# The first two blocks of values from the unscaled input, and the order of the first loads

## The chip, the cores and the metric

The kernel runs on one core of a Trainium2 chip. The metric is the time of one execution on the device in microseconds (us); lower is better. TensorE multiplies matrices, ScalarE and VectorE work on tiles in SBUF and PSUM, GpSimd does little here, and SyncE issues loads. TensorE's clock has two levels, 1.2 and 2.4 GHz; the profile tells which was granted.

## The reference

With the given sizes the model is one layer: a root-mean-square norm, one input projection, stick-breaking attention with 16 heads of 64, a gate, an output projection, the residual and a final norm.

```python
def rmsnorm(x, g):
    y = xf * lax.rsqrt(jnp.mean(xf * xf, axis=-1, keepdims=True) + EPS)
    return (y * g)
def mixer_stick_breaking(h, w_in, w_out):      # x: 2048 x 1024 float32, w_in: 1024 x 4096
    proj = jnp.einsum('bsd,de->bse', h, w_in)
    q, k, v, g = jnp.split(proj, 4, axis=-1)
    o = stick_breaking_attention(q.reshape(hs), k.reshape(hs), v.reshape(hs))
    return jnp.einsum('bse,ed->bsd', o * jax.nn.silu(g), w_out)
x = x + mixer_stick_breaking(rmsnorm(x, a_norm[j]), a_w_in[j], a_w_out[j])
return rmsnorm(x, final_norm)
```

## The kernel before

All products are made from high and low parts: a float32 tile a is split into a_hi (rounded for the matmul) and a_lo = a - a_hi, and a product is a_hi b_hi + a_hi b_lo + a_lo b_hi. ScalarE makes a high part, VectorE the low part from it.

**The value stage** comes first. The 2048 tokens are 16 blocks of 128 (NB), the model width 8 slices of 128 (KT). A value block v (32 of them: 16 token blocks times two halves of the 1024 value columns) is 8 x 3 matmuls of 128 x 512 into one of two PSUM tiles (proj_ps), lines 524 to 530. For token block s the stage needs:

- x_rows (x, line 376, two buffers), of which ScalarE takes the sum of squares (`square`), VectorE the mean (`mean`), ScalarE the root (`root`), and VectorE five small operations (`chain`) the scale of each token;
- `turn_scale`: TensorE multiplies the scale, broadcast along 128 columns, by the identity, so that it lies along the tokens in a spare PSUM tile;
- x_T (the transposed input, line 381, three buffers), which VectorE multiplies by the turned scale in place (`scaled`), and which is then split into hT_hi (`h_hi`) and hT_lo (`h_lo`). These stay for all later projections;
- the value weights, 8 slices in four quarters a half (wv_raw, line 384), multiplied by a_norm as they are split (`wv_high`, `wv_low`).

ScalarE copies a finished value block from PSUM to v_stage (`empty_v`, line 664) and issues its stores, one or two. The order of each engine's queue is written out by hand: after the first blocks all run in rounds s, in which ScalarE does root(s+2), h_hi(s), square(s+3), empty_v(s-2), and VectorE scaled(s), chain(s+2), h_lo(s), mean(s+3). TensorE's block v waits for h_lo(v) and for empty_v(v-2), and has turn_scale(v+2) in its middle. SyncE issues the loads in order, and waits where a buffer is not free:

```python
                def load_x(s):
                    if s >= 2:
                        sp.wait_ge(s_sumsq, s - 1)
                def load_xT(s):
                    if s >= 3:
                        sp.wait_ge(s_hlo, s - 2)
```

from block 4 on xT(s) and then x(s+1), with a quarter of the second half's weights after s = 7, 9, 11 and 13.

Behind it come the projections of queries, keys and gates, woven into 640 steps of attention, and the output (to 1715 us). Their instructions are not touched.

## Time and profile before

| | |
|---|---|
| median of 3 runs | 1716.97 us (1715.53 to 1718.01) |
| the profiled execution | 1717.58 us |
| its span, first to last instruction | 1715.6 us |
| TensorE busy | 1660.1 us (97%) |
| VectorE busy | 1307.8 us (76%) |
| ScalarE busy | 873.5 us (51%) |
| granted TensorE clock, mean | 0.991 of full |
| DMA | 216.08 MB, 126 GB/s on average |

Shares are averages over stages with different limits. The value stage is the first 204 us. A row of a timeline gives start and duration in us, engine, source line, operation, output and input, the number merged, and in brackets how long the engine stood idle before it and what ended that. Matmuls are pipelined: their durations overlap, so the pace is read from starts.

### The profile page before, as it was taken

What the parts mean: (1) busy time and instruction counts of PE and PEld (TensorE: products, weight loads), DVE (VectorE), ACT (ScalarE), POOL (GpSimd) and SP (SyncE); (2) the same over time, 40 slices, a digit from 0 to 9 for tenths busy, and PEclk for the clock granted to TensorE, in tenths of its full rate; (3) what the DMA queues carried; (4) which work ended last, traced back from release to release, by engine and by line L of the source; (5) the groups of instructions that cost most, each with busy time, mean ns of one, the idle gap of its engine ahead of it and who ended that gap; (6) DMA issues with size and microseconds to landing.
All of it is one profiled execution on the core that took longest, in us unless ns stands there. A gap on an engine that the chain in (4) does not pass through costs nothing. (4 is left out here: it accounts for less than half of the span.)

```text
span 1715.6 us, 23382 instructions
## 1 busy us (share of the span) xinstructions
PE 1660.1 (97%) x8600; PEld 1381.8 (81%) x8600; DVE 1307.8 (76%) x1855; ACT 873.5 (51%) x1730; POOL 230.0 (13%) x212
## 2 busy tenths in 40 slices
PE   5999999999999999999999999999999999989988
PEld 4778878888888888888888888888888888768776
DVE  5530058889888888888888888888888989955564
ACT  5431145556555565555565655555555656631221
POOL 0010012011111011201210211011101120003331
PEclk9999999999999999999999999999999999989999
DMA  6832243343524243333333341524243435456553
GB/s 247 277 97 50 70 135 119 115 118 95 157 69 136 65 149 94 105 99 111 109 101 111 99 142 57 147 85 134 81 119 105 115 96 177 142 178 227 200 199 110
DMA packets 156974, 216.08 MB, mean 126 GB/s; under 512 B 49088, under 2 KB 90048, under 8 KB 156864
## 3 DMA queue, kind: packets, MB, share of 16 engines
q1 hardware_dynamic: 87376, 139.05, 26.4%
q10 hardware_dynamic: 69488, 75.58, 14.7%
q8 instruction: 67, 1.10, 0.3%
q14 instruction: 43, 0.35, 0.1%
HBM read 139.01 MB, written 75.56 MB: 125 GB/s over the span
## 5 line engine op out<-in xcount | busy, mean ns | idle before, releaser
L711 ACT ACTIVATE u<-z_ps 128x512 f32<-128x512 f32 (+3 forms) x640 | 341.3, 533 | 413.8 <-PE z_ps L588 411.8
L885 DVE TENSOR_TENSOR_SCAN u<-u,u 128x512 f32<-128x512 f32 x384 | 490.8, 1278 | 0.0
L890 DVE TENSOR_TENSOR r_turned_lo<-turn_ps,r_turned_hi 128x512 fp32r<-128x512 f32 (+3 forms) x640 | 376.0, 588 | 35.4 <-ACT r_turned_hi L717 34.0
L717 ACT ACTIVATE r_turned_hi<-turn_ps 128x512 fp32r<-128x512 f32 (+3 forms) x640 | 339.8, 531 | 64.0 <-issue 45.0
L597 PE MATMUL turn_ps<-ident,u 128*128 128x128 f32 x2176 | 344.8, 274 | 0.0
L510 POOL TENSOR_SCALAR w_raw<-w_raw,a_norm_col 128x128 f32<-128x128 f32 x192 | 177.7, 943 | 1216.5 <-DMA w_raw<-in_w_qkg 1216.5
L570 PE MATMUL proj_ps<-hT_lo,w_hi 128*128 128x512 f32 x768 | 320.4, 417 | 0.0
L570 PE MATMUL proj_ps<-hT_hi,w_hi 128*128 128x512 f32 x768 | 320.1, 417 | 0.0
L570 PE MATMUL proj_ps<-hT_hi,w_lo 128*128 128x512 f32 x768 | 319.2, 416 | 0.0
L597 PEld LDWEIGHTS turn_ps<-ident,u 128*128 128x128 f32 x2176 | 269.3, 141 | 59.0 <-issue 0.4
L611 PE MATMUL o_ps<-r_turned_hi,dv_head 128*128 128x512 f32 (+3 forms) x640 | 233.2, 364 | 14.7 <-DVE r_turned_lo L890 13.1
L587 PE MATMUL z_ps<-k_parts,q_parts 128*128 128x512 f32 (+3 forms) x640 | 234.1, 366 | 0.3 <-ACT u L711 0.3
L588 PE MATMUL z_ps<-k_parts,q_swapped 128*128 128x512 f32 (+3 forms) x640 | 234.2, 366 | 0.0
L612 PE MATMUL o_ps<-r_turned_lo,dv_head 128*128 128x512 f32 (+3 forms) x640 | 232.9, 364 | 0.0
L885 DVE TENSOR_TENSOR_SCAN u<-u,unbroken 128x512 f32<-128x512 f32 (+3 forms) x256 | 210.1, 822 | 0.0
L611 PEld LDWEIGHTS o_ps<-r_turned_hi,dv_head 128*128 128x128 f32 x640 | 120.4, 188 | 51.9 <-DVE r_turned_lo L890 19.5
L570 PEld LDWEIGHTS proj_ps<-hT_hi,w_lo 128*128 128x128 f32 x768 | 145.5, 190 | 16.4
L570 PEld LDWEIGHTS proj_ps<-hT_lo,w_hi 128*128 128x128 f32 x768 | 145.6, 190 | 15.9
L570 PEld LDWEIGHTS proj_ps<-hT_hi,w_hi 128*128 128x128 f32 x768 | 145.4, 189 | 15.5
L871 DVE TENSOR_TENSOR made_lo<-proj_ps,made_hi 128x512 fp32r<-128x512 f32 x64 | 44.2, 690 | 144.9 <-ACT made_hi L692 144.9
L612 PEld LDWEIGHTS o_ps<-r_turned_lo,dv_head 128*128 128x128 f32 x640 | 120.8, 189 | 27.4
L587 PEld LDWEIGHTS z_ps<-k_parts,q_parts 128*128 128x128 f32 x640 | 120.4, 188 | 20.6 <-ACT u L711 1.0
(89 smaller groups left out, 1657.3 us busy)
## 6 DMA issues: line engine op xcount, KB each, us to landing
qk_hi_cols<-made_hi ACTq DMA_DIRECT2D x64, 256.0 KB, 2.8
qk_lo_cols<-made_lo ACTq DMA_DIRECT2D x64, 256.0 KB, 3.4
w_raw<-in_w_qkg SPq DMA_DIRECT2D x24, 512.0 KB, 3.6
x_rows<-in_x SPq DMA_DIRECT2D x16, 512.0 KB, 5.3
x_T<-in_xT SPq DMA_DIRECT2D x16, 512.0 KB, 4.4
v_rows<-v_stage ACTq DMA_DIRECT2D x32, 256.0 KB
v_here<-v_rows SPq DMA_DIRECT2D x64, 128.0 KB, 2.7
v_next<-v_rows SPq DMA_DIRECT2D x64, 128.0 KB, 2.9
```

The source lines that it names most:

```text
L510: last = nc.gpsimd.tensor_scalar(w_raw[t % 2][:, k, :], w_raw[t % 2][:, k, :], norm_col[:, k:k + 1], None, ALU.mult)
L570: last = nc.tensor.matmul(p_ps[g % RP][:], a[t % 2][:, k, :], b[:, c, k, :], start=(n == 0), stop=(n == QPM - 1))
L587: nc.tensor.matmul(out, q_parts[c % 2][:, tau], k_parts[:, sig], start=True, stop=False)
L588: nc.tensor.matmul(out, q_swapped[c % 2][:, tau], k_parts[:, sig], start=False, stop=True).then_inc(s_z, 1)
L597: last = nc.tensor.transpose(t_ps[m % RT][:, t * P:(t + 1) * P], u_t[unit][t][:, r * P - lo:(r + 1) * P - lo], ident[:])
L611: nc.tensor.matmul(o_ps[:, 0:w], weights, rt_hi[m % RT][:, 0:w], start=begin, stop=False)
L612: last = nc.tensor.matmul(o_ps[:, 0:w], weights, rt_lo[m % RT][:, 0:w], start=False, stop=end)
L711: nc.scalar.activation(u_t[(m // CB) % RU][STEPS[m][3]][:, 0:w], z_ps[m % RZ][:, 0:w], ACT.Sigmoid, scale=-Z_SCALE).then_inc(s_u, 1)
L717: nc.scalar.activation(rt_hi[m % RT][:, 0:w], t_ps[m % RT][:, 0:w], ACT.Copy).then_inc(s_hi, 1)
L871: nc.vector.tensor_tensor(made_lo[:], p_ps[g % RP][:], as_f32(made_hi[:]), ALU.subtract).then_inc(s_plo, 1)
L885: nc.vector.tensor_tensor_scan(u, u, other, start, ALU.mult, op).then_inc(s_r, 1)
L890: nc.vector.tensor_tensor(rt_lo[m % RT][:, 0:w], t_ps[m % RT][:, 0:w], as_f32(rt_hi[m % RT][:, 0:w]), ALU.subtract).then_inc(s_lo, 1)
```

## The change

For token blocks 0 and 1 (EARLY = 2) xT is split without the scale (`stage_hi`, `stage_lo`) into four new tiles, which lie where the second half's weights come later. Value blocks 0 and 1 are made from these, and ScalarE multiplies them by the token scale as it copies them out of PSUM (there the scale is one number a partition). The scaled parts of blocks 0 and 1 are still needed for value blocks 16 and 17 and for all other projections; they are made after those of block 2. `made(s)` is the place of block s in the order 2, 0, 1, 3, 4, .... The loads begin with xT(0), a_norm, the first quarter of the weights, xT(1), the other three quarters, and only then x(0) and x(1).

```diff
@@ -209,6 +209,17 @@
+EARLY = 2
+MADE = [EARLY] + list(range(EARLY)) + list(range(EARLY + 1, NB))
+def made(s):
+    return MADE.index(s) + 1
 CHAIN = 5
...
@@ -248,6 +259,8 @@
         xrow = [place(nc, f"x_rows{n}", [P, D], F32, at) for n, at in enumerate(AT_XROW)]
+        st_hi = [place(nc, f"unscaled_hi{n}", [P, KT, P], F32R, AT_WV[1][0] + 4 * KB * n) for n in range(EARLY)]
+        st_lo = [place(nc, f"unscaled_lo{n}", [P, KT, P], F32R, AT_WV[1][1] + 4 * KB * n) for n in range(EARLY)]
         vst = [place(nc, f"v_stage{n}", [P, HD], F32, AT_VST + 2 * KB * n) for n in range(2)]
...
@@ -302,6 +315,8 @@
         s_row = sem("scale_turned")
+        s_sthi = sem("unscaled_hi_ready")
+        s_stlo = sem("unscaled_lo_ready")
         s_scaled = sem("xT_scaled")
...
@@ -377,7 +392,7 @@
                     if s >= 3:
-                        sp.wait_ge(s_hlo, s - 2)
+                        sp.wait_ge(s_hlo, made(s - 3))
                     sp.dma_start(xt[s % 3][:], xT[s]).then_inc(s_xT[s % 3], 16)
...
@@ -414,17 +429,16 @@
-                load_x(0)
                 load_xT(0)
...
                 load_wv(0, 0)
+                load_xT(1)
+                for q in range(1, KT // 2):
+                    load_wv(0, q)
+                load_x(0)
                 load_x(1)
-                load_xT(1)
-                load_wv(0, 1)
-                load_wv(0, 2)
+                load_xT(2)
                 load_x(2)
-                load_wv(0, 3)
-                load_xT(2)
                 load_x(3)
...
@@ -432,6 +446,8 @@
                         load_x(s + 1)
+                    if s == 7:
+                        sp.wait_ge(s_v, EARLY)
                     if s in (7, 9, 11, 13):
...
@@ -517,35 +533,37 @@
                     if s >= len(row_ps):
-                        pe.wait_ge(s_scaled, s - len(row_ps) + 1)
+                        pe.wait_ge(s_scaled, made(s - len(row_ps)))
                     nc.tensor.transpose(row_ps[s % len(row_ps)][:, 0:P], scale[:, s:s + 1].to_broadcast([P, P]),
...
                     f, (c, tok) = v // NB, block_of(v % NB)
+                    hi, lo = (hT_hi[:, c, :, tok], hT_lo[:, c, :, tok]) if v >= EARLY else (st_hi[v][:], st_lo[v][:])
                     for k in ks:
-                        for n, (a, b) in enumerate(((hT_hi, wv_hi[f]), (hT_hi, wv_lo[f]), (hT_lo, wv_hi[f]))):
-                            last = nc.tensor.matmul(p_ps[v % 2][:], a[:, c, k, tok], b[:, k, :],
+                        for n, (a, b) in enumerate(((hi, wv_hi[f]), (hi, wv_lo[f]), (lo, wv_hi[f]))):
+                            last = nc.tensor.matmul(p_ps[v % 2][:], a[:, k, :], b[:, k, :],
                                                     start=(k == 0 and n == 0), stop=(k == KT - 1 and n == 2))
...
                 pe.wait_ge(s_ident, 2)
-                turn_scale(0)
-                turn_scale(1)
                 for q in range(KT // 2):
                     pe.wait_ge(s_wvlo, q + 1)
-                    for v in range(2):
+                    for v in range(EARLY):
                         if q == 0:
-                            pe.wait_ge(s_hlo, v + 1)
+                            pe.wait_ge(s_stlo, v + 1)
                         last = products(v, range(2 * q, 2 * q + 2))
...
                             last.then_inc(s_v, 1)
-                    if q >= 2:
-                        turn_scale(q)
-                for v in range(2, 2 * NB):
+                            if v == 0:
+                                for s in range(EARLY + 1):
+                                    turn_scale(s)
+                turn_scale(EARLY + 1)
+                for v in range(EARLY, 2 * NB):
                     if v < NB:
-                        pe.wait_ge(s_hlo, v + 1)
+                        pe.wait_ge(s_hlo, made(v))
                     if v == NB:
+                        pe.wait_ge(s_hlo, NB)
                         pe.wait_ge(s_wvlo, KT)
...
@@ -647,8 +665,12 @@
                     c, tok = block_of(s)
-                    act.wait_ge(s_scaled, s + 1)
+                    act.wait_ge(s_scaled, made(s))
                     nc.scalar.activation(hT_hi[:, c, :, tok], xt[s % 3][:], ACT.Copy).then_inc(s_hhi, 1)
+                def stage_hi(s):
+                    act.wait_ge(s_xT[s % 3], 16)
+                    nc.scalar.activation(st_hi[s][:], xt[s % 3][:], ACT.Copy).then_inc(s_sthi, 1)
...
@@ -661,7 +683,11 @@
                         v_stored(act, v - 2)
-                    nc.scalar.activation(vst[v % 2][:], p_ps[v % 2][:], ACT.Copy).then_inc(s_vst, 1)
+                    if v < EARLY:
+                        act.wait_ge(s_chain, CHAIN * (v + 1))
+                        nc.scalar.activation(vst[v % 2][:], p_ps[v % 2][:], ACT.Copy, scale=scale[:, v:v + 1]).then_inc(s_vst, 1)
+                    else:
+                        nc.scalar.activation(vst[v % 2][:], p_ps[v % 2][:], ACT.Copy).then_inc(s_vst, 1)
                     act.wait_ge(s_vst, v + 1)
...
@@ -743,26 +769,25 @@
-                square(0)
-                root(0)
-                square(1)
-                root(1)
+                stage_hi(0)
                 act.wait_ge(s_norm, 16)
                 wv_high(0, 0)
+                stage_hi(1)
+                for q in range(1, KT // 2):
+                    wv_high(0, q)
+                for s in range(EARLY + 1):
+                    square(s)
+                    root(s)
+                h_hi(EARLY)
+                square(EARLY + 1)
                 h_hi(0)
-                wv_high(0, 1)
+                root(EARLY + 1)
                 h_hi(1)
-                wv_high(0, 2)
-                square(2)
-                wv_high(0, 3)
-                root(2)
-                square(3)
-                root(3)
-                square(4)
+                square(EARLY + 2)
                 for s in range(2, 2 * NB + 2):
...
                         root(s + 2)
-                    if s < NB:
+                    if EARLY < s < NB:
                         h_hi(s)
...
@@ -833,9 +858,13 @@
                     c, tok = block_of(s)
-                    dve.wait_ge(s_hhi, s + 1)
+                    dve.wait_ge(s_hhi, made(s))
                     nc.vector.tensor_tensor(hT_lo[:, c, :, tok], xt[s % 3][:], as_f32(hT_hi[:, c, :, tok]),
                                             ALU.subtract).then_inc(s_hlo, 1)
+                def stage_lo(s):
+                    dve.wait_ge(s_sthi, s + 1)
+                    nc.vector.tensor_tensor(st_lo[s][:], xt[s % 3][:], as_f32(st_hi[s][:]), ALU.subtract).then_inc(s_stlo, 1)
...
@@ -906,24 +935,26 @@
                 nc.vector.memset(zeros[:], 0.0).then_inc(s_zero, 1)
-                mean(0)
-                chain(0)
-                mean(1)
-                chain(1)
+                stage_lo(0)
+                wv_low(0, 0)
+                stage_lo(1)
+                for q in range(1, KT // 2):
+                    wv_low(0, q)
+                for s in range(EARLY + 1):
+                    mean(s)
+                    chain(s)
+                scaled(EARLY)
                 scaled(0)
-                wv_low(0, 0)
+                h_lo(EARLY)
+                scaled(1)
+                mean(EARLY + 1)
                 h_lo(0)
-                scaled(1)
-                wv_low(0, 1)
+                chain(EARLY + 1)
                 h_lo(1)
-                wv_low(0, 2)
-                mean(2)
-                wv_low(0, 3)
-                chain(2)
-                mean(3)
-                chain(3)
-                mean(4)
-                for s in range(2, NB):
+                mean(EARLY + 2)
+                chain(EARLY + 2)
+                mean(EARLY + 3)
+                for s in range(EARLY + 1, NB):
                     scaled(s)
...
                         chain(s + 2)
```

**ScalarE, from the squares of block 2 or 3 to the first copy out of PSUM.** Before (x_T_66 is block 2; v_stage_69 takes value block 0; the x_rows alternate, so the last squares ahead of the copy are block 5's):

```order
L642 ACTIVATE square_junk,stat<-x_rows_67 128x1024 [waits sum_squares_ready,x_loaded0]
L646 ACTIVATE stat<-stat 128x1 [waits mean_square_ready]
L651 ACTIVATE hT_hi<-x_T_66 128x8x128 [waits xT_scaled]
L642 ACTIVATE square_junk,stat<-x_rows_68 128x1024 [waits sum_squares_ready,x_loaded1]
L664 ACTIVATE v_stage_69<-proj_ps 128x512 [waits v_ready]
L668 DMA v_rows<-v_stage_69 128x8x64 [waits v_evacuated]
L646 ACTIVATE stat<-stat 128x1 [waits mean_square_ready]
```

and with the change, from the squares of block 2 on:

```order
L660 ACTIVATE square_junk,stat<-x_rows_67 128x1024 [waits sum_squares_ready,x_loaded0]
L664 ACTIVATE stat<-stat 128x1 [waits mean_square_ready]
L669 ACTIVATE hT_hi<-x_T_66 128x8x128 [waits xT_scaled]
L660 ACTIVATE square_junk,stat<-x_rows_68 128x1024 [waits sum_squares_ready,x_loaded1]
L669 ACTIVATE hT_hi<-x_T_64 128x8x128 [waits xT_scaled]
L664 ACTIVATE stat<-stat 128x1 [waits mean_square_ready]
L669 ACTIVATE hT_hi<-x_T_65 128x8x128 [waits xT_scaled]
L660 ACTIVATE square_junk,stat<-x_rows_67 128x1024 [waits sum_squares_ready,x_loaded0]
L664 ACTIVATE stat<-stat 128x1 [waits mean_square_ready]
L660 ACTIVATE square_junk,stat<-x_rows_68 128x1024 [waits sum_squares_ready,x_loaded1]
L688 ACTIVATE v_stage_73<-proj_ps,token_scale 128x512 [waits rms_chain,v_ready]
L694 DMA v_rows<-v_stage_73 128x8x64 [waits v_evacuated]
```

Squares 2, 3 and 4 stood ahead of the high part of block 2 and only squares 5 behind it; now the high parts of blocks 2, 0 and 1 (x_T_66, x_T_64, x_T_65) and squares 3, 4 and 5 all stand between squares 2 and the copy of block 0.

**SyncE, the loads after the first ones.** Before, from x(2) to x(5):

```order
L376 DMA x_rows_67<-in_x 128x1024 [waits sum_squares_ready]
L384 DMA wv_raw_62<-in_w_v 128x1024
L381 DMA x_T_66<-in_xT 128x1024
L376 DMA x_rows_68<-in_x 128x1024 [waits sum_squares_ready]
L381 DMA x_T_64<-in_xT 128x1024 [waits hT_lo_ready]
L376 DMA x_rows_67<-in_x 128x1024 [waits sum_squares_ready]
L381 DMA x_T_65<-in_xT 128x1024 [waits hT_lo_ready]
L376 DMA x_rows_68<-in_x 128x1024 [waits sum_squares_ready]
```

and with the change, from the last three quarters of the first weights to x(4) and xT(4):

```order
L399 DMA wv_raw_62<-in_w_v 128x1024 x3
L391 DMA x_rows_67<-in_x 128x1024
L391 DMA x_rows_68<-in_x 128x1024
L396 DMA x_T_66<-in_xT 128x1024
L391 DMA x_rows_67<-in_x 128x1024 [waits sum_squares_ready]
L391 DMA x_rows_68<-in_x 128x1024 [waits sum_squares_ready]
L396 DMA x_T_64<-in_xT 128x1024 [waits hT_lo_ready]
L391 DMA x_rows_67<-in_x 128x1024 [waits sum_squares_ready]
L396 DMA x_T_65<-in_xT 128x1024 [waits hT_lo_ready]
L391 DMA x_rows_68<-in_x 128x1024 [waits sum_squares_ready]
```

x(0) and x(1) moved behind all first weights. The first x_T that waits (x_T_64, block 3) waits for the low part of block 0, which is now the second made.

**VectorE and TensorE behind the scales.** VectorE with the change, from the end of the third chain:

```order
L857 TENSOR_TENSOR x_T_66<-x_T_66,turn_ps 128x1024 [waits scale_turned,xT_loaded2,rms_chain]
L857 TENSOR_TENSOR x_T_64<-x_T_64,z_ps 128x1024 [waits scale_turned,xT_loaded0]
L862 TENSOR_TENSOR hT_lo<-x_T_66,hT_hi 128x8x128 [waits hT_hi_ready]
L857 TENSOR_TENSOR x_T_65<-x_T_65,z_ps 128x1024 [waits scale_turned,xT_loaded1]
L847 TENSOR_SCALAR stat<-stat 128x1 [waits sum_squares_ready]
L862 TENSOR_TENSOR hT_lo<-x_T_64,hT_hi 128x8x128 [waits hT_hi_ready]
```

TensorE with the change, from the last matmul of value block 0:

```order
L545 MATMUL proj_ps<-wv_hi_58,unscaled_lo_71 128x512
L537 MATMUL z_ps<-ident,token_scale 128x128 [waits rms_chain] x2
L537 MATMUL turn_ps<-ident,token_scale 128x128 [waits rms_chain]
L545 MATMUL proj_ps<-wv_hi_58,unscaled_hi_70 128x512
L545 MATMUL proj_ps<-wv_lo_60,unscaled_hi_70 128x512
```

The low part of block 0 is the sixth of these operations, and the scales of blocks 0, 1 and 2 are turned between the value blocks 0 and 1, where before the turns of 0 and 1 came ahead of all products.

## Rows read from the trace of the kernel before

**Rows 1.** Busy time by stretch (us, engines, TensorE clock, DMA share, GB/s).

```profile
30.49:60.00 29.51, 28.11 (x123) 22.32 (x124) 17.13 (x41) 14.05 (x25) 0.00 (x0) 1.00 0.86 263
93.00:106.00 13.00, 13.00 (x52) 10.41 (x53) 8.15 (x13) 5.65 (x9) 0.00 (x0) 0.87 0.42 103
106.00:203.80 97.80, 97.80 (x433) 81.00 (x432) 4.67 (x5) 14.15 (x22) 9.31 (x16) 1.00 0.25 60
```

**Rows 2.** Who waited for whom, TensorE, whole span (us in total, times, longest).

```profile
PE proj_ps L528 <- ACT v_stage L664: 6.4, 6, 1.8
```

**Rows 3.** Timeline of TensorE: first matmuls of blocks 0, 2 and 12.

```profile
15.71 0.77 PE L528 MATMUL proj_ps<-wv_hi,hT_hi 128*128 128x512 f32 x1 [3.33 <-DVE hT_lo L837]
...
30.49 0.47 PE L528 MATMUL proj_ps<-wv_hi,hT_hi 128*128 128x512 f32 x1 [1.23 <-ACT v_stage L664]
...
92.86 0.47 PE L528 MATMUL proj_ps<-wv_hi,hT_hi 128*128 128x512 f32 x1 [1.80 <-ACT v_stage L664]
```

**Rows 4.** Timeline of ScalarE, 28.5 to 31.5 us and at 203.8.

```profile
28.73 1.04 ACT L642 ACTIVATE square_junk<-x_rows 128x1024 bf16<-128x1024 f32 x1
...
29.77 0.57 ACT L664 ACTIVATE v_stage<-proj_ps 128x512 f32<-128x512 f32 x1
...
30.86 0.20 ACT L646 ACTIVATE stat<-stat 128x1 f32<-128x1 f32 x1 [0.52 <-ACT v_stage L664]
31.38 1.06 ACT L651 ACTIVATE hT_hi<-x_T 128x1024 fp32r<-128x1024 f32 x1 [0.31 <-DVE x_T L832]
...
203.85 0.60 ACT L664 ACTIVATE v_stage<-proj_ps 128x512 f32<-128x512 f32 x1 [4.84 <-PE proj_ps L528]
```

**Rows 5.** Who waited for whom, ScalarE, 30 to 106 us.

```profile
ACT square_junk L642 <- DMA x_rows<-in_x: 15.4, 8, 3.3
```

**Rows 6.** Timeline of VectorE: the low parts of blocks 0, 1, 2, 3 and 4.

```profile
14.34 1.22 DVE L837 TENSOR_TENSOR hT_lo<-x_T,hT_hi 128x1024 fp32r<-128x1024 f32 x1
...
17.93 1.22 DVE L837 TENSOR_TENSOR hT_lo<-x_T,hT_hi 128x1024 fp32r<-128x1024 f32 x1
...
28.93 1.23 DVE L837 TENSOR_TENSOR hT_lo<-x_T,hT_hi 128x1024 fp32r<-128x1024 f32 x1 [0.35 <-ACT hT_hi L651]
...
32.95 1.22 DVE L837 TENSOR_TENSOR hT_lo<-x_T,hT_hi 128x1024 fp32r<-128x1024 f32 x1 [0.76 <-ACT hT_hi L651]
...
40.39 1.23 DVE L837 TENSOR_TENSOR hT_lo<-x_T,hT_hi 128x1024 fp32r<-128x1024 f32 x1
```

**Rows 7.** Timeline of SyncE, 30 to 31 us.

```profile
30.18 0.33 SPq L381 DMA_DIRECT2D x_T<-in_xT  x1
30.55 0.43 SPq L376 DMA_DIRECT2D x_rows<-in_x  x1
```

**Rows 8.** DMA issues between 30.1 and 30.9 us: KB, us to landing.

```profile
x_T<-in_xT SPq DMA_DIRECT2D x1, 512.0 KB, 3.8
x_rows<-in_x SPq DMA_DIRECT2D x1, 512.0 KB, 5.2
```

**Rows 9.** DMA issues between 0.7 and 1.2 us.

```profile
x_rows<-in_x SPq DMA_DIRECT2D x1, 512.0 KB, 3.6
```

**Rows 10.** DMA issues between 5.95 and 6.5 us.

```profile
wv_raw<-in_w_v SPq DMA_DIRECT2D x1, 512.0 KB, 9.6
```

**Rows 11.** Timeline of ScalarE, 5 to 12 us.

```profile
5.60 1.28 ACT L646 ACT_TABLE_LOAD   x1
6.89 0.20 ACT L646 ACTIVATE stat<-stat 128x1 f32<-128x1 f32 x1
9.23 1.06 ACT L642 ACTIVATE square_junk<-x_rows 128x1024 bf16<-128x1024 f32 x1 [2.13 <-DMA x_rows<-in_x]
...
10.78 1.32 ACT L656 ACTIVATE wv_hi<-wv_raw,a_norm_col 128x512 fp32r<-128x512 f32 x2
```

**Rows 12.** Timeline of VectorE, 11 to 15 us.

```profile
11.68 0.16 DVE L226 TENSOR_TENSOR token_scale<-token_scale,stat 128x1 f32<-128x1 f32 x1
...
13.02 1.41 DVE L843 SCALAR_TENSOR_TENSOR wv_lo<-wv_raw,a_norm_col,wv_hi 128x512 fp32r<-128x512 f32 x2
```

## The prediction

> **What bounds the kernel now.** I read the stretches first, then who waited for whom, then the timelines around the places where TensorE stood. From 106 to 203.8 us TensorE never rests: 433 matmuls in 97.8 us, 0.226 us each, so a value block of 24 costs 5.42 us [rows 1]. That is the pace it could hold throughout. From 30.49 to 60 us it is busy for only 28.11 of 29.51 us [rows 1]. In the whole span TensorE waits 6.4 us, in 6 waits, for the copies of values out of PSUM (v_stage, line 664) [rows 2]. It begins its first block at 15.71, block 2 at 30.49 and block 12 at 92.86 us [rows 3]; the last block leaves PSUM at 203.85 [rows 4]. From 30.49 to 92.86 are 10 blocks, 6.24 us each, against 5.42. After 92.86 it is only TensorE. So **the end of the value stage is set by when block 12 may start**, and all later work follows it one for one.
>
> Who sets the 6.24? ScalarE's queue. In round s it does root(s+2), the high part of block s, the squares of block s+3, and only then empties block s-2 [rows 4]. The squares wait for rows of x: 15.4 us in 8 waits between 30 and 106 us [rows 5]. The rows come late because SyncE's queue is in order: x(s+3) stands behind xT(s+2), which waits for the low part of block s-1, whose buffer it takes. The low part of block 2 ends at 30.15 (28.93 + 1.22) [rows 6]; xT(5) and x(6) are issued at 30.18 and 30.55 [rows 7] and land 3.8 and 5.2 us later [rows 8]. So there is a loop: h_lo(s-1), load x(s+3) 5.6, squares 1.0, empty 0.6 with its DMA issues 1.1, root and high part 1.2, low part 1.2 gives h_lo(s+1). That makes 11 to 12 us for two blocks: h_lo ends at 30.15, 34.17 and 41.62 [rows 6], 11.5 from the first to the third. Two such chains, of even and odd blocks, take turns.
>
> **The change, part by part.**
> - Loads. Nine loads of 512 KB, with the small a_norm between them, land between 4.4 us (0.8 + 3.6) [rows 9] and 15.6 (6.0 + 9.6) [rows 10]: one per 1.4. In the new order the places are xT(0) 4.4, the four quarters of the weights and xT(1) up to 11.5, x(0) about 13, x(1) 14.2, xT(2) 15.6.
> - First products. Splitting xT(0) costs 1.06 + 1.22, the first weights 1.32 on ScalarE and 1.41 on VectorE [rows 6, 11, 12]. Weights landed at 6.6 give a start near 9 to 9.5 us instead of 15.71, 6 us earlier. 48 matmuls, some eight of them at the lower clock, and the turns: both blocks are done by 23 us, before by 29.3 (block 2's start less its wait of 1.23) [rows 3].
> - Scales. They now come last. Squares of x(0) end at 14.2, the table load takes 1.28 [rows 11], squares of x(1) end near 17. x(2) can't be issued before 14.2 and lands 3.6 later, 17.8. From the start of its squares to the end of its chain takes 2.6 (9.23 to 11.84) [rows 11, 12]: 20.5. That meets TensorE after block 0 (42 matmuls from 9.4: 20.7), so the wait put between block 0 and block 1 is 0 to 0.5 us, hidden by what follows.
> - Blocks 0 and 1 still need scaled parts for the later projections, and now they are made behind block 2's. VectorE has scaled(2), scaled(0), low(2), scaled(1), low(0), five passes of 1.15 and a wait of 1.0 for ScalarE's high part, from 21.1: **h_lo(0) ends near 27.5** (before 15.56), h_lo(1) a chain and a pass later, 29.7 (before 19.15) [rows 6].
> - What that frees. xT(3) waits for h_lo(0), x(4) is queued behind it: issued at 27.9, landed at 32.7 (xT(3) 3.8 after its issue at 27.5 and one place of 1.4; the 5.2 of rows 8 has a store of values beside it, here none is out yet). Behind it stand xT(4), released at 29.7, and x(5): two more places, 35.4. In the kernel before, x(4) and x(5) were long there.
> - The emptying of block 0 stands behind squares(4) and squares(5) on ScalarE. 35.4 + 1.04 + 0.57 and 0.15 to TensorE (30.49 against 29.77 + 0.57) [rows 3, 4]: **block 2 starts near 37.0 instead of 30.49, 6.5 us later**. So the 6 us won at the start lie in front of a wait of some 14 us (23 to 37, broken only by the turn of scale 3) and are worth nothing.
> - How it goes on. mean(5) now stands ahead of scaled(3) on VectorE, so h_lo(3) follows squares(5): 36.6, scaled 1.2, high 1.1, low 1.2, near 40.2 (before 34.17, +6.0). h_lo(4) follows the emptying of block 1, near 44.3 (before 41.62, +2.7) [rows 6]. These are the starts of the two chains. Their loads share one queue, so the later one pushes the other: the shift settles between 2.7 and 6.0. I take 4.5, the middle, since block 12 waits for x(15), whose place in the queue both have touched; that puts block 12 near 97.4 instead of 92.86. If TensorE alone decided, block 2 plus ten at 5.42 would put block 12 at 91.2; the loop's 6.24 is longer, so the loop decides.
> - The new scaled copy of v_stage replaces a plain one twice, and the wait ahead of the next load of weights is long met when it comes: nothing.
>
> The sum: 4.5 us on top of the profiled execution's 1717.58, whose span is 1715.6: 1722.1. That run is 0.6 above the median of 1716.97, so **1721.5**.
>
> A rule to weigh. The table load is 1.28 us, from 5.60, with the root right behind it at 6.89, and it stands now on the way to x(1)'s squares [rows 11]. The Trainium skill (ScalarE: Activation LUTs, What ACT_TABLE_LOAD costs) gives 1283 ns and another 1380 ns of drain per switch. By that the squares of x(1) would end at 18.3 instead of 17, 0.5 past the landing of x(2), and the estimate would be 0.5 us more; the trace shows no such second part.
>
> **The rivals.**
> 1. The shift is mostly swallowed: 0 to 3.4 us, about 1719. The less delayed chain (+2.7) decides, or the fall of the clock between 93 and 106 us (0.87 on average over 13 us, so 1.7 us lost [rows 1]) does not come again. For: both are of the size. Against: h_lo(3) is far behind and its chain feeds the same queue.
> 2. Faster: from block 2 on TensorE sets the pace. Needs the loads to keep up, since without the early loads nothing is squeezed together: x(4) and x(5) each 3.6 us after their issue and block 2 at 35.3. Then 30 blocks of 5.42 and 1.7 at the lower clock end at 199.6 against 203.8, 4.2 less, 1713. It decides if the loop's round falls under 5.42. Against: it is 6.24 now, and the same loads, passes and copies stand in it.
> 3. Slower by more: 7 to 10 us, 1725. Over 14 us of waiting the clock falls to 1.2 GHz and block 2 starts there; as rows 1 show for 93 to 106 us it costs 1.7, which delays the turn of scale 4 and with it h_lo(4), and both chains run at +6. The Trainium skill (TensorE: Matmul & The Clock Gate, HAM oscillation) says that waiting for DMA brings the engine back to the slow clock, burst after burst; by that I would add 1.7 for each further long wait. Before, the first waits of 1.2 us did not show a lower clock in the row of 30.49 to 60 us.
> 4. The change does not start the products early, because the weights land no sooner. The end stays as worked out: the path does not run through them.
>
> **How the numbers follow.** A measurement here can tell about 0.2%, 3.4 us, from no change. The forecast (+3.4 to +7) gets 0.62, rival 1 0.23, rival 2 0.07, rival 3 0.08. Faster 0.06, since rival 2 can fall short of 3.4; same 0.24; slower 0.70. The range that holds 8 in 10 reaches from +0.8 into rival 1 to +8.5 into rival 3: 1717.8 to 1725.5.
>
> **What would show it.** First product near 9.4 us; squares(4) and squares(5) waiting for x; xT(3) issued near 27.5; block 2 near 37; then 5.4 to 6.3 us a block, and the last v_stage near 208. Wrong if the last v_stage is at or before 204, or if block 2 starts before 33.

## The result, and the profile after

| | before | with the change |
|---|---|---|
| median of 5 runs | 1717.13 us (1715.53 to 1719.57) | 1725.10 us (1724.06 to 1730.15) |
| ratio | | 1.0051, 95% interval 1.0034 to 1.0069 |
| profiled execution | 1717.58 us | 1724.06 us |
| its span | 1715.6 us | 1722.3 us |

Slower by 8.0 us, half a per cent, where 4.5 were forecast. The way was right and the size was not: 1725.1 is just inside the range given, but the ratio of 1.0051 on 1716.97 is 1725.7 and just outside it. All times and ratios below are of fast runs: one execution each of e3, e8 and e10 took 1900 to 2765 us at a much lower granted clock and is left out.

The stretches of the new kernel (columns as in [rows 1]): ahead of the start of block 2, from there until the loads end, and TensorE alone.

```profile
10.83:40.25 29.42, 14.28 (x53) 11.04 (x53) 17.26 (x45) 16.01 (x28) 0.00 (x0) 0.81 0.56 205
40.25:106.00 65.75, 63.17 (x267) 50.72 (x268) 38.19 (x91) 32.73 (x58) 0.00 (x0) 0.95 0.77 229
114.00:211.50 97.50, 97.50 (x432) 80.77 (x431) 5.09 (x5) 14.45 (x23) 9.30 (x16) 1.00 0.25 60
```

From 114 us on it is the pace of before, 432 matmuls in 97.5 us. The first stretch holds 14.28 us of work in 29.42 and a mean clock of 0.81. Who waited for whom on TensorE [rows 2], the whole span:

```profile
PE proj_ps L545 <- DVE wv_lo L872: 10.8, 1, 10.8
PE proj_ps L545 <- ACT v_stage L688: 9.6, 1, 9.6
...
PE turn_ps L537 <- DVE token_scale L237: 5.5, 1, 5.5
PE proj_ps L545 <- ACT v_stage L690: 2.6, 2, 1.8
```

One wait of 9.6 us for the copy of block 0 (line 688) and one of 5.5 for the fourth scale take the place of the small ones. The timeline of TensorE at those places [rows 3]:

```profile
10.83 0.76 PE L545 MATMUL proj_ps<-wv_hi,unscaled_hi 128*128 128x512 f32 x1 [10.83 <-DVE wv_lo L872]
...
22.96 0.27 PE L537 MATMUL turn_ps<-ident,token_scale 128*128 128x128 f32 x1
...
30.16 0.48 PE L537 MATMUL turn_ps<-ident,token_scale 128*128 128x128 f32 x1 [5.54 <-DVE token_scale L237]
40.25 0.76 PE L545 MATMUL proj_ps<-wv_hi,hT_hi 128*128 128x512 f32 x1 [9.61 <-ACT v_stage L688]
```

Block 0 starts 4.9 us earlier than before, block 2 9.8 us later. Block 12 stands behind the last such wait:

```profile
102.12 0.47 PE L545 MATMUL proj_ps<-wv_hi,hT_hi 128*128 128x512 f32 x1 [1.81 <-ACT v_stage L690]
```

9.3 us later than in [rows 3]. ScalarE at the squares of x(0), x(4), x(5), the copy of block 0, and the last copy [rows 4]:

```profile
14.34 1.06 ACT L660 ACTIVATE square_junk<-x_rows 128x1024 bf16<-128x1024 f32 x1
...
34.42 1.06 ACT L660 ACTIVATE square_junk<-x_rows 128x1024 bf16<-128x1024 f32 x1 [5.11 <-DMA x_rows<-in_x]
...
38.38 1.06 ACT L660 ACTIVATE square_junk<-x_rows 128x1024 bf16<-128x1024 f32 x1 [2.38 <-DMA x_rows<-in_x]
...
39.43 0.67 ACT L688 ACTIVATE v_stage<-proj_ps,token_scale 128x512 f32<-128x512 f32 x1
```

```profile
211.56 0.60 ACT L690 ACTIVATE v_stage<-proj_ps 128x512 f32<-128x512 f32 x1 [4.84 <-PE proj_ps L545]
```

Squares(4) and (5) wait 5.11 and 2.38 us for their rows of x, and the copy of block 0, ready since 23 us, is behind them. The last copy is at 211.56 instead of 203.85: **the value stage is 7.7 us longer, and that is the whole effect.** What follows took 1510.7 us here and 1511.7 before.

Of the 9.3 us at block 12, 1.6 are won back behind it, because the kernel before has a stretch at the lower clock there (94.2 to 97.7 us) and the changed one has none. And from block 4 to block 10 TensorE waits for nothing. The first row is the changed kernel over blocks 4 to 9, 5.59 us each and no idle time; the other two are the kernel before, over blocks 4 to 8 and over blocks 9 to 11:

```profile
54.39:87.95 33.56, 33.56 (x151) 27.38 (x150) 20.11 (x45) 17.11 (x30) 0.00 (x0) 1.00 0.85 250
43.26:71.67 28.41, 28.24 (x126) 22.68 (x125) 15.61 (x40) 14.24 (x26) 0.00 (x0) 1.00 0.97 298
71.67:92.86 21.19, 17.45 (x76) 13.38 (x75) 12.64 (x29) 10.51 (x19) 0.00 (x0) 1.00 0.59 190
```

So the 6.24 us a block of the prediction are a mean. TensorE's own pace with a turn in each block is 5.59; before, 3.7 of the waits stand ahead of blocks 10, 11 and 12, and 1.23 each ahead of blocks 2 and 3. ScalarE's waits for x [rows 5], 30 to 106 us:

```profile
ACT square_junk L660 <- DMA x_rows<-in_x: 17.5, 9, 5.1
```

VectorE's low parts [rows 6], in the order 2, 0, 1, 3, 4, and the scaling of block 4:

```profile
25.71 1.22 DVE L862 TENSOR_TENSOR hT_lo<-x_T,hT_hi 128x1024 fp32r<-128x1024 f32 x1
...
28.05 1.22 DVE L862 TENSOR_TENSOR hT_lo<-x_T,hT_hi 128x1024 fp32r<-128x1024 f32 x1
...
30.14 1.23 DVE L862 TENSOR_TENSOR hT_lo<-x_T,hT_hi 128x1024 fp32r<-128x1024 f32 x1
...
42.15 1.23 DVE L862 TENSOR_TENSOR hT_lo<-x_T,hT_hi 128x1024 fp32r<-128x1024 f32 x1 [0.35 <-ACT hT_hi L669]
...
46.02 1.22 DVE L857 TENSOR_TENSOR x_T<-x_T,z_ps 128x1024 f32<-128x1024 f32 x1 [2.58 <-PE z_ps L537]
...
48.44 1.22 DVE L862 TENSOR_TENSOR hT_lo<-x_T,hT_hi 128x1024 fp32r<-128x1024 f32 x1 [0.35 <-ACT hT_hi L669]
```

h_lo(0) ends at 29.27 and h_lo(1) at 31.37 (before 15.56 and 19.15), h_lo(3) at 43.38 and h_lo(4) at 49.66. SyncE acts on each at once [rows 7]:

```profile
29.29 0.33 SPq L396 DMA_DIRECT2D x_T<-in_xT  x1
29.66 0.43 SPq L391 DMA_DIRECT2D x_rows<-in_x  x1
31.40 0.33 SPq L396 DMA_DIRECT2D x_T<-in_xT  x1
31.77 0.43 SPq L391 DMA_DIRECT2D x_rows<-in_x  x1
```

and the landings of the last pair (xT(4) and x(5)) [rows 8]:

```profile
x_T<-in_xT SPq DMA_DIRECT2D x1, 512.0 KB, 5.7
x_rows<-in_x SPq DMA_DIRECT2D x1, 512.0 KB, 6.6
```

### The profile page after: what moved, and what is told of

Read it like the earlier page. It is cut to its first block and busy times, and to the rows that moved or that the text cites. A ratio compares the mean times of both kernels' runs of the same rounds, so it can differ in the third digit from the quotient of the medians.

```text
span 1722.3 us, 23387 instructions
## 1 busy us (share of the span) xinstructions
PE 1660.1 (96%) x8600; PEld 1382.8 (80%) x8600; DVE 1313.3 (76%) x1857; ACT 876.6 (51%) x1732; POOL 231.5 (13%) x212
## 5 line engine op out<-in xcount | busy, mean ns | idle before, releaser
L630 PEld LDWEIGHTS o_ps<-r_turned_lo,dv_head 128*128 128x128 f32 x640 | 120.8, 189 | 27.5
```

Source lines behind the costliest of these rows:

```text
L630: last = nc.tensor.matmul(o_ps[:, 0:w], weights, rt_lo[m % RT][:, 0:w], start=False, stop=end)
```

## The experiments

Each kernel was timed against the kernel before. Since one execution's remainder behind the value stage varies by some us (1510.7 to 1516.0 over the profiled executions here) whatever was edited, the place of the last copy out of PSUM in the value stage tells an edit better than the total; the one kernel profiled twice (e7 and e7b) gave 198.72 and 198.37. Only the kernel before has the stretch at the lower clock behind block 12: from the start of block 12 to the last v_stage it takes 111.0 us, all others 109.3 to 109.4, so against the kernel before the start of block 12 compares better. The start of block 0 too varies, from 9.5 to 11.1 us over the kernels that keep the change's first loads, with the landing of the first weights.

| kernel | block 0 starts | block 2 starts | h_lo(3), h_lo(4) end | block 4 starts | block 12 starts | last v_stage | ratio to before (95%) |
|---|---|---|---|---|---|---|---|
| before | 15.71 | 30.49 | 34.17, 41.62 | 43.26 | 92.86 | 203.85 | 1 |
| the change | 10.83 | 40.25 | 43.38, 49.66 | 54.39 | 102.12 | 211.56 | 1.0051 (1.0034 to 1.0069) |
| e1 loads only | 22.65 | 37.47 | 41.16, 48.61 | 50.25 | 100.77 | 210.20 | 1.0051 (1.0034 to 1.0069) |
| e2 x first | 10.90 | 39.99 | 43.12, 48.51 | 52.94 | 101.89 | 211.31 | 1.0030 (1.0016 to 1.0043) |
| e3 empty first | 10.08 | 28.98 | 42.19, 45.80 | 50.57 | 98.55 | 207.98 | 1.0018 (1.0005 to 1.0031) |
| e4 two x ahead | 10.22 | 33.15 | 36.28, 45.41 | 47.03 | 96.55 | 205.98 | 0.9997 (0.9987 to 1.0008) |
| e5 keep clock | 11.09 | 40.08 | 43.20, 49.49 | 54.08 | 102.33 | 211.74 | 1.0039 (1.0028 to 1.0050) |
| e5b clock kept | 10.96 | 39.76 | 42.89, 47.39 | 51.03 | 99.69 | 209.12 | 1.0030 (1.0017 to 1.0042) |
| e6 turns earlier | 10.64 | 38.26 | 41.39, 46.59 | 51.04 | 99.16 | 208.57 | 1.0013 (1.0003 to 1.0023) |
| e7 rows first, before | 16.15 | 33.36 | 37.06, 41.04 | 44.67 | 89.41 | 198.72 | 0.9959 (0.9944 to 0.9974) |
| e7b the same again | 15.80 | 33.05 | 36.74, 40.72 | 44.32 | 89.06 | 198.37 | 0.9954 (0.9940 to 0.9968) |
| e8 rows first, change | 10.23 | 34.91 | 38.04, 44.33 | 48.77 | 93.52 | 202.82 | 0.9990 (0.9980 to 1.0000) |
| e9 late xT(4), before | 15.75 | 39.07 | 42.62, 48.50 | 53.15 | 101.46 | 210.87 | 1.0033 (1.0022 to 1.0044) |
| e10 repaired change | 9.50 | 28.31 | 36.26, 40.85 | 42.08 | 86.83 | 196.13 | 0.9957 (0.9943 to 0.9971) |

From block 4 to block 12 the kernels with the old order of x(s+1) and xT(s) take 47.7 to 50.5 us, and those with the new one (e7, e7b, e8, e10) 44.7. So an edit ahead of block 4 shows at block 12 within 2 us as it shows at block 4.

### e1: the new order of the loads, alone

```diff
 # before.py, SyncE
-load_x(0); load_xT(0); norm; load_wv(0, 0); load_x(1); load_xT(1); load_wv(0, 1); load_wv(0, 2); load_x(2); load_wv(0, 3); load_xT(2)
+load_xT(0); norm; load_wv(0, 0); load_xT(1); load_wv(0, 1..3); load_x(0); load_x(1); load_xT(2); load_x(2)
```

> The kernel before with nothing but the new order of the first loads. Theory L (the late scales of blocks 0 and 1 shift the loop of x loads): x(0) lands at 14.3 instead of 4.4, so the scales of blocks 0 and 1 and their low parts come some 7 to 10 us late; block 0 starts near 22, block 2 near 36.5, the last v_stage near 210 (the change: 211.6), 5 to 7 us slower than before. Rival P (what hurts is that the unscaled blocks push the scaled parts of 0 and 1 and the turns behind them, and the order of the loads is harmless): last v_stage within 1 us of 203.9.

Last v_stage 210.20: the loads alone cost 6.4 of the 7.7 us (at block 12, 7.9 of 9.3). TensorE waits 17.4 us for the first scale:

```profile
PE z_ps L520 <- DVE token_scale L226: 18.4, 2, 17.4
PE proj_ps L527 <- ACT v_stage L663: 7.1, 5, 1.8
```

### e2: the change, x(0) and x(1) first in the loads

```diff
 # after.py, SyncE
+load_x(0); load_xT(0); norm; load_wv(0, 0); load_x(1); load_xT(1); load_wv(0, 1..3); load_xT(2); load_x(2)
```

> The change with x(0) first again in the loads (x(0), xT(0), a_norm, a quarter, x(1), xT(1), three quarters, xT(2), x(2)). Theory L: ScalarE does its squares behind all weights whatever has landed, and the weights land one or two places later, so the squares of x(2) and h_lo(0) come at the same time or up to 1 us later than in the change: block 2 near 40 to 41, last v_stage 211 to 213. Rival (the order of the loads alone costs the 7.7 us): last v_stage near 204 to 206.

211.31, as the change. So the two parts don't add: each alone makes the scales late, the loads because x lands late, ScalarE's order because the squares stand behind the weights (here the squares of x(0) start at 15.66 us, right behind the last weights, though its load was the first). Giving back one of them gives back nothing.

### e3: blocks 0 and 1 copied out ahead of the squares that wait

```diff
 # after.py, ScalarE
                 h_hi(1)
+                empty_v(0)
                 square(EARLY + 2)
...
+                    if s == 2:
+                        empty_v(1)
                     if s + 3 < NB:
                         square(s + 3)
-                    empty_v(s - 2)
+                    if s > 3:
+                        empty_v(s - 2)
```

> The change with blocks 0 and 1 copied out of PSUM ahead of squares(4) and squares(5) on ScalarE. Theory L: block 2 starts near 31 instead of 40.3, 9 us earlier, and the last v_stage stays within 1.5 us of 211.6, since the loop of x loads sets block 12. Rival E (the wait of 9.6 us ahead of block 2 is itself the loss): the last v_stage comes 6 to 9 us earlier, near 203 to 205.

Block 2 starts 11.3 us earlier and the stage ends 3.6 earlier, of which up to 0.75 may be the earlier start of this execution. Neither figure holds: more than the 1.5 that I allowed, far less than the wait of 9.6. TensorE's time comes back as new waits, first for the scale of block 4, whose squares wait for x(4), then for h_lo(3):

```profile
28.85 0.48 PE L537 MATMUL turn_ps<-ident,token_scale 128*128 128x128 f32 x1 [5.53 <-DVE token_scale L237]
...
35.86 0.32 PE L537 MATMUL z_ps<-ident,token_scale 128*128 128x128 f32 x1 [1.43 <-DVE token_scale L237]
...
42.24 0.79 PE L545 MATMUL proj_ps<-wv_hi,hT_hi 128*128 128x512 f32 x1 [3.30 <-DVE hT_lo L866]
```

The wait of 3.30 us for h_lo(3), which itself is only 1.2 us earlier, and a lower clock in blocks 2 and 3 (0.61 on average from 28.98 to 35.80, 0.66 from 42.20 to 50.57) leave 3.8 us at block 4 (50.57 instead of 54.39), and these reach the end. So an early block 2 alone is lost again at block 3, whose low part hangs on the late loads.

### e5 and e5b: TensorE kept busy in its wait

```diff
 # after.py, TensorE
+                for _ in range(32):                    # e5b: 48
+                    nc.tensor.transpose(t_ps[2][:, 0:P], ident[:], ident[:])
                 turn_scale(EARLY + 1)
+                for _ in range(56):                    # e5b: 86
+                    nc.tensor.transpose(t_ps[2][:, 0:P], ident[:], ident[:])
```

> The change with 32 and 56 transposes of the identity into an unused PSUM tile where TensorE waits between blocks 1 and 2 (extra work, no result of it is used), so that its clock stays up. Theory L: the turn of scale 4 in the middle of block 2 comes 2.6 us earlier and h_lo(4) with it (47 instead of 49.7), but the last v_stage moves by less than 1 us from 211.6, since the other chain of loads is as late. Rival C (the lower clock after the long wait is what made the loss larger than forecast): last v_stage 2 to 3 us earlier, near 209.

The edit missed its aim: the transposes ran out at 36.5 us, TensorE stood 3.54 us more, its clock was low from 39.1 us, and block 2 ran slow as without them. It serves as the control for the next run, with more of them:

> As the run with the 32 and 56 transposes, where TensorE still stood 3.5 us ahead of block 2 and its clock was low from 39.1 to 45.9 us; now 48 and 86, which fill the wait. Theory L: if the clock stays up, the turn of scale 4 comes 2.6 us after the start of block 2 instead of 5.3, h_lo(4) near 47, and the last v_stage still within 1 us of 211.6. Rival C (the clock's cost is carried through): last v_stage 2 to 3 us earlier, near 209.

Now the clock stays at 2.4 GHz through block 2, and the turn of scale 4 comes 2.8 us after the start of block 2 (39.76); the scaling of block 4 follows at 42.95, not at 46.02:

```profile
39.76 0.47 PE L546 MATMUL proj_ps<-wv_hi,hT_hi 128*128 128x512 f32 x1
...
42.57 0.27 PE L538 MATMUL z_ps<-ident,token_scale 128*128 128x128 f32 x1
```

```profile
42.95 1.22 DVE L862 TENSOR_TENSOR x_T<-x_T,z_ps 128x1024 f32<-128x1024 f32 x1
...
46.16 1.23 DVE L867 TENSOR_TENSOR hT_lo<-x_T,hT_hi 128x1024 fp32r<-128x1024 f32 x1
```

The stage ends 2.4 us earlier (2.6 against e5): **rival C holds**, and my theory's "within 1 us" falls. Block 2 takes 5.68 us instead of 8.55 (first row the change, second e5b):

```profile
40.25:48.80 8.55, 8.55 (x26) 6.74 (x26) 4.99 (x15) 4.13 (x7) 0.00 (x0) 0.64 0.67 185
39.76:45.44 5.68, 5.68 (x26) 4.64 (x27) 4.18 (x11) 3.41 (x7) 0.00 (x0) 1.00 0.41 110
```

These 2.9 us, and 0.5 of an earlier start of block 2, are still there in full at block 9 (79.00 instead of 82.36), since TensorE waits for nothing between; the waits ahead of blocks 10 to 12 take 0.9 of the 3.4 back. The early turn is thus not what carries it: from block 3 to block 9 every low part is ready 2.5 us or more ahead of its block, in both kernels. The ratio, 1.0030 against 1.0051, has intervals that overlap.

### e6: the turns of the scales ahead of block 0's last quarter

```diff
 # after.py, TensorE
                     for v in range(EARLY):
+                        if (q, v) == (KT // 2 - 1, 0):
+                            for s in range(EARLY + 1):
+                                turn_scale(s)
...
-                            if v == 0:
-                                for s in range(EARLY + 1):
-                                    turn_scale(s)
```

> The change with the turns of the scales of blocks 0, 1 and 2 ahead of the last quarter of block 0 on TensorE instead of behind it. In the change the third turn ran at 22.96 us, 1.5 us after its scale was ready (21.44), and the scaled blocks began at 23.37. Theory L: h_lo(0) and all behind it come 1.3 to 1.5 us earlier, and so does the last v_stage: 210.0 to 210.5. Rival (this step has slack): last v_stage within 0.5 us of 211.6, counted from the same start of block 0.

The third turn runs at 21.23 after a wait of 0.30, h_lo(0) ends at 27.59, 1.7 us earlier, and the stage ends 3.0 earlier, twice what was expected. This step had no slack. What makes 3.0 of it shows in block 2: it starts 2.0 us earlier (38.26), and it takes 7.18 us instead of 8.55, because the clock is back at 2.4 GHz 3.1 us after its start and not 6.2:

```profile
38.26:45.44 7.18, 7.18 (x25) 5.72 (x26) 4.71 (x15) 4.14 (x7) 0.00 (x0) 0.78 0.61 157
```

Of these 3.4 us 3.0 reach block 12.

### e4: x(4) and x(5) ahead of the transposed block 3

```diff
 # after.py, SyncE
                 load_x(3)
-                load_xT(3)
                 load_x(4)
+                load_x(5)
+                load_xT(3)
                 for s in range(4, NB):
                     load_xT(s)
-                    if s + 1 < NB:
+                    if 4 < s < NB - 1:
```

> The change with x(4) and x(5) issued ahead of xT(3), which waits for h_lo(0). Theory L: x(4) and x(5) land near 25 and 31 instead of 34.4 and 38.4, block 2 starts near 34 instead of 40.3, and this shift stays: the last v_stage near 207.5 (3.5 to 5 us less than 211.6). Rival (the late transposed blocks xT(3) and xT(4) themselves hold the stage, not the rows queued behind them): last v_stage within 1 us of 211.6.

205.98: 5.6 of the 7.7 us come back, a little more than the 3.5 to 5 expected, with two loads moved past one that waits. Nothing was saved in work or bytes.

### e9: one late load, put into the kernel before

```diff
 # before.py, SyncE, load_xT
-                        sp.wait_ge(s_hlo, s - 2)
+                        sp.wait_ge(s_hlo, 3 if s == 4 else s - 2)
```

> The kernel before, in which only xT(4), and x(5) behind it, waits for the low part of block 2 (30.2 us) instead of that of block 1 (19.2). Theory L: this one wait repeats the harm: x(5) lands near 36, block 2 starts near 37 instead of 30.5, last v_stage 4 to 6 us later, near 208 to 210. Rival (the harm needs the unscaled blocks, the clock or the new order of operations): last v_stage within 1 us of 203.9.

210.87, 7.0 us later (8.6 at block 12), more than the 4 to 6 expected, with the first products and all queues of the engines as before. As in the change, the clock falls in the long wait and block 2 takes 8.48 us, so this run shows the late load and the slow block that comes of it together. TensorE's wait is the change's in small:

```profile
PE proj_ps L528 <- ACT v_stage L664: 10.3, 3, 7.3
```

A load that waits, with the rows of x behind it in SyncE's queue, is enough for the harm.

### e7 and e8: x(s+1) ahead of xT(s) throughout

```diff
 # before.py (e7) and after.py (e8), SyncE
                 load_x(3)
-                load_xT(3)
                 load_x(4)
+                load_xT(3)
                 for s in range(4, NB):
-                    load_xT(s)
                     if s + 1 < NB:
                         load_x(s + 1)
+                    load_xT(s)
```

> The kernel before with x(s+1) issued ahead of xT(s) from s = 3 on, nothing else. Theory L (x behind xT behind the low part makes the round of 6.2 us a block): the waits for x on ScalarE nearly go, TensorE runs at 5.44 us a block, block 12 starts near 87.5 instead of 92.9, the last v_stage near 197 to 198.5 and the time 5 to 7 us below the kernel before. Rival (the DMA engines are full in this stage, so x only trades places with xT): last v_stage within 1.5 us of 203.9.

198.72 and 0.9959 of the kernel before, 7 us below it. From block 2 to block 12 it takes 5.6 us a block, not the 5.44 that I expected (the turn in the middle of each block costs TensorE the rest), and block 12 starts at 89.41, 3.45 us earlier, though block 2 started 2.9 later. Of the 6.3 us by which these ten blocks are shorter, 4.4 lie in blocks 9 to 11, where the waits of the kernel before stand; at the last v_stage 1.6 more come from its stretch at the lower clock, which does not occur here. Behind a single wait of 1.23 us at block 2 TensorE waits for no copy any more; from 30 to 106 us ScalarE waits for x no more, and for the scaled block instead, which TensorE's pace sets:

```profile
PE proj_ps L528 <- ACT v_stage L664: 1.2, 1, 1.2
```

```profile
ACT hT_hi L651 <- DVE x_T L832: 22.4, 11, 4.7
```

> The change with x(s+1) issued ahead of xT(s) from s = 3 on. Theory L: x(4) comes early but x(5) still waits its turn, block 2 near 37 to 38, then TensorE's own pace: last v_stage near 204 to 205, so 7 us below the change and about level with the kernel before, and 6 to 7 us above the kernel before with the same edit. Rival (the start 5 us earlier is now worth something, because the pace is TensorE's): last v_stage at or below that of the kernel before with this edit, 197.

202.82: 8.7 us below the change and 4.1 above e7; I had expected 204 to 205, 6 to 7 above e7, with block 2 at 37 to 38. With a start 5.9 us earlier than e7's, block 2 still begins 1.6 later, and from there neither waits. The other 2.5 us are the clock: in e8 it is low until 40.5 us, and block 2's first thirteen matmuls take 0.43 us each instead of 0.23 (the first row is e8 from the start of block 2, the second e7):

```profile
34.91:40.50 5.59, 5.59 (x14) 4.32 (x15) 2.70 (x8) 3.04 (x6) 0.00 (x0) 0.51 0.88 266
```

```profile
33.36:40.00 6.64, 6.64 (x30) 5.41 (x31) 4.96 (x15) 4.23 (x8) 0.00 (x0) 1.00 0.81 260
```

### e10: the change with everything mended

```diff
 # after.py with e3, e6 and
                 load_x(3)
+                load_x(4)
+                load_x(5)
                 load_xT(3)
-                load_x(4)
...
+                scaled(EARLY + 1)
                 mean(EARLY + 3)
                 for s in range(EARLY + 1, NB):
-                    scaled(s)
+                    if s > EARLY + 1:
+                        scaled(s)
```

and x(s+1) ahead of xT(s) for s > 4.

> The change with all that the runs found: x(s+1) ahead of xT(s), x(5) ahead of xT(3), the turns of 0 to 2 ahead of block 0's last quarter, blocks 0 and 1 copied out ahead of squares(4) and (5), scaled(3) ahead of the mean of block 5. Theory L: block 2 starts near 28.5 to 29.5, but block 3 still waits for h_lo(3), near 36 to 37, since x(4) and the scale of block 3 come late; last v_stage 199 to 201, 0 to 2 us behind the kernel before with rows first (198.7). Rival (the start 5 us earlier pays once the loads are out of the way): last v_stage below 197.

> The kernel before with x(s+1) ahead of xT(s), once more on the same chip as the repaired change: last v_stage 198 to 199, 5 to 8 us below the kernel before.

196.13 against 198.37 for e7b, in times 1712.5 and 1712.1 us (medians), and ratios 0.9957 and 0.9954. In the stage my theory (199 to 201) fell and its rival held (below 197: the early start pays once the loads are out of the way); in the whole time nothing shows, since 2.2 us are less than the executions of either kernel differ by (4.9 and 6.1 us). Block 0 of e10 started 0.6 us earlier than in any other kernel with its loads, and that may be part of the 2.2. A first product 6.3 us earlier returns 2.2 at most, and only with four other edits; the order of two loads returned 5.1 and 5.5 alone. The theory had block 3 right, which waits for h_lo(3) at 36.3:

```profile
36.31 0.50 PE L546 MATMUL proj_ps<-wv_hi,hT_hi 128*128 128x512 f32 x1 [0.56 <-DVE hT_lo L867]
```

## Why the prediction was wrong

- **That the early start is worth nothing**, because x(4), x(5) and with them block 2 come late behind loads that wait for a buffer: right. Block 0 started 4.9 us earlier and nothing of it was left in the end, and e9 repeats the harm without it.
- **"The loop's 6.24 is longer, so the loop decides"**: this step failed as a mechanism. It compares 6.24, a mean over ten blocks with all their waits, with 5.42, TensorE's pace without turns. With its turns TensorE takes 5.59 a block, and in the change nothing holds it up between the start of block 2 and block 10; the loop of loads tells only ahead of block 2 and again from 10 to 12. So the late block 2 is not evened out between two chains but carried on: block 4 starts 11.1 us later than before, block 9 10.7, block 12 9.3. In size this step erred least: a block 2 at 37.0 with the clock up, followed by the 59.0 us that the change takes from there to block 12 without the 2.9 of the slow block, gives 96.0, 3.1 later than before, where the sum had 4.5.
- **The start near 9 to 9.5**: 10.83. The first weights landed at 7.8 us (issued at 1.72, 6.1 us), not at 6.6, and all that lands later came with them: x(0) at 14.3 (4.29 + 10.0) instead of 13, x(2) at 18.8 instead of 17.8. This term was a uniform 1.4 us per place; the first places took longer.
- **"0 to 0.5 us, hidden by what follows"** for the wait between blocks 0 and 1: wrong in sign and size. The scale was ready at 21.44, and the turn stood behind block 0's last matmuls until 22.96. It delayed VectorE by 1.5 us, and e6 shows that nothing hid it: 3.0 us at the end.
- **h_lo(0) near 27.5, h_lo(1) 29.7**: 29.27 and 31.37, 1.8 and 1.7 late, by the two terms above.
- **x(4) at 32.7, x(5) at 35.4**: 34.4 (when the squares begin) and 38.37 (31.77 + 6.6). The first is late with h_lo(0). For the second I gave xT(4) one place of 1.4; it took 5.7 us from its issue, with no store beside it.
- **Block 2 near 37.0**: 40.25, the sum of these: 3.3 us, the largest term that was mis-sized.
- **The lower clock, priced at 1.7 us in rival 3 and at nothing in the sum**: the step that failed in size. At the start of block 2 the granted clock was low, for the 12 matmuls of 0.43 us up to the turn and two behind it, and the block took 2.9 us more than at 2.4 GHz (e5b: 5.68 instead of 8.55). I gave rival 3 only 0.08, and let it work through the turn of scale 4. h_lo(4) did come at 49.66 instead of 44.3, 3.3 us from block 2's late start and some 2 from the clock; but no block waited for it, and the loss went through TensorE's own time. The Trainium skill (TensorE: Matmul & The Clock Gate, HAM oscillation), cited in that rival, has waits for DMA bring the slow clock back. The trace agrees for the long waits ahead of block 2. The waits of 1.8 us further on are shorter than those it describes, and went both ways: the clock stayed up behind the one of 1.81 at 102 us, and before it fell behind one of 1.80 at 92.86.
- **The shift settles between +2.7 and +6.0, so 4.5**: it was +9.8 at block 2 and +9.3 at block 12. The middle of two chains was no rule, and its two ends were 5.3 and 3.2 us short (+8.0 and +9.2 measured for h_lo(4) and h_lo(3)). The sum that the runs give is 3.1 (above), 3.3 for the later block 2 and 2.9 for the clock, 9.3 at block 12, less the 1.6 of the stretch at the lower clock that only the kernel before has behind it: 7.7.
- Rival 1 had one half right: the fall of the clock between 93 and 106 us did not come again, and the stage ended only 7.7 us later where block 12 was 9.3 later. Of rival 2 the condition held (from block 2 on TensorE set the pace, up to block 10), but from a block 2 that came 9.8 us late, so nothing was gained.
- The table load: 1.28 us, from 15.51, and the root at 16.80, as before. The second part that the Trainium skill (ScalarE: Activation LUTs, What ACT_TABLE_LOAD costs) adds does not show here either:

```profile
15.51 1.28 ACT L664 ACT_TABLE_LOAD   x1
16.80 0.20 ACT L664 ACTIVATE stat<-stat 128x1 f32<-128x1 f32 x1
```

## What to carry to other kernels

An engine that starts earlier gains only if what it waits for next comes earlier too; find the last wait ahead of the stretch that runs without waits, and follow it back through the buffers that are given free, not only through the data. In an in-order queue of loads, one that waits for a buffer holds up all behind it, so the load whose buffer comes free first belongs first: that swap alone was worth 0.4%. Before a mean round is called the pace of a loop, look at the blocks one by one: here most ran at TensorE's own pace and a few held all the waits. And a long new wait on TensorE has to be priced with the slow block behind it, 2.9 us here, which nothing takes back as long as TensorE sets the pace.

## What the runs showed of the hardware that was not expected

- Three loads of 512 KB issued within 0.9 us at 31.4 us took 5.7, 6.6 and 7.4 us, while the pair issued from 29.29 on took 3.9 and 4.7. The first store of values was issued only at 40.13; what slowed the three was not tried.
- 56 transposes of 128 x 128 until 36.5 us and a wait of 3.54 did not keep the clock of block 2 up; 86 that ran into it did. In the change it fell at 29.4 us, 4.7 us after TensorE's last matmul of block 1, and was low until 46.4.
- The same first loads started block 0 anywhere between 9.5 and 11.1 us.
